# Scan of the even layer: order of VectorE's instructions within a step

## The reference, cut to what matters

```python
def rwkv7_scan(r, w, k, v, kk, bb, s0, reverse):
    def step(s, inp):
        r_t, w_t, k_t, v_t, kk_t, b_t = inp
        sa = jnp.einsum('bhij,bhj->bhi', s, kk_t)
        s = s * w_t[:, :, None, :] - sa[..., None] * b_t[:, :, None, :] + v_t[..., None] * k_t[:, :, None, :]
        return s, jnp.einsum('bhij,bhj->bhi', s, r_t)
...
    for d in range(2):
...
        s_ctx, yc = rwkv7_scan(*tc[:6], zeros, d == 1)
        _, yl = rwkv7_scan(*tl[:6], s_ctx, d == 1)
```

## Time and profile before

| | |
|---|---|
| median of 3 executions | 3216.98 us (3214.37 to 3218.5) |
| span of the profiled execution | 3213.7 us |
| TensorE, share of the span | 95% |
| VectorE | 54% |
| ScalarE | 36% |
| GpSimd | 42% |

### The profile page before, as it was taken

The page is one execution under the profiler, slowest core; times in us unless marked ns, Lnnn a source line. Parts: engine busy times, 40 slices in busy tenths (PEclk is TensorE's granted clock), DMA queues, the critical chain, the costliest instruction groups (busy, mean ns, idle before and its releaser), DMA issues. The chain is left out here.

```text
span 3213.7 us, 52487 instructions
## 1 busy us (share of the span) xinstructions
PE 3045.3 (95%) x20065; PEld 2461.7 (77%) x20065; DVE 1728.6 (54%) x3224; ACT 1155.9 (36%) x2075; POOL 1349.1 (42%) x893
## 2 busy tenths in 40 slices
PE   5999999899999999999999999999888889999998
PEld 4888876678887888877788887987666667778887
DVE  6445478654445566232666114537677754674443
ACT  3222235432223322234332223226544434435343
POOL 3444443244444434453434444224767660143332
PEclk8999999999999999999999999999999999999999
DMA  7655432155544554332255334213222233222222
GB/s 216 195 184 173 158 85 73 53 170 183 183 156 153 167 180 135 97 90 79 86 163 151 94 93 136 79 53 112 65 58 58 56 107 73 91 77 71 82 66 59
DMA packets 641381, 366.02 MB, mean 114 GB/s; under 512 B 107902, under 2 KB 634132, under 8 KB 640688
## 3 DMA queue, kind: packets, MB, share of 16 engines
q1 hardware_dynamic: 633216, 351.57, 37.2%
q10 hardware_dynamic: 6640, 10.49, 1.1%
q0 software_dynamic: 1344, 1.44, 0.2%
HBM read 334.27 MB, written 24.97 MB: 112 GB/s over the span
## 5 line engine op out<-in xcount | busy, mean ns | idle before, releaser
L270 POOL TENSOR_TENSOR w_lo<-w_raw,w_hi 128x1024 fp32r<-128x1024 f32 (+1 forms) x333 | 786.6, 2362 | 1316.6 <-ACT w_hi L262 1263.9
L335 PE MATMUL acc<-h,w_hi 128*128 128x512 f32 x2256 | 704.4, 393 | 0.0
L262 ACT ACTIVATE w_hi<-w_raw 128x1024 fp32r<-128x1024 f32 (+1 forms) x332 | 344.6, 1038 | 941.1 <-PE acc L335 687.9
L335 PEld LDWEIGHTS acc<-h,w_hi 128*128 128x128 f32 x2256 | 417.3, 188 | 84.6 <-issue 1.8
L335 PE MATMUL acc<-h,w_lo 128*128 128x512 f32 x1128 | 440.3, 390 | 0.0
L335 PE MATMUL acc<-hid,w_hi 128*128 128x512 f32 x1056 | 326.3, 390 | 0.0
L716 DVE SCALAR_TENSOR_TENSOR ada_part<-ada_raw,c_act,ada_part 128x256 f32<-128x256 f32 x672 | 315.0, 489 | 18.6
L335 PEld LDWEIGHTS acc<-h,w_lo 128*128 128x128 f32 x1128 | 211.7, 188 | 45.8
L335 PEld LDWEIGHTS acc<-hid,w_hi 128*128 128x128 f32 x1056 | 197.3, 188 | 40.7
L335 PE MATMUL spare<-h,w_hi 128*128 128x512 f32 x688 | 211.7, 389 | 0.0
L335 PE MATMUL acc<-hid,w_lo 128*128 128x512 f32 x528 | 205.6, 389 | 0.0
(11 more groups left out here) (700 smaller groups left out, 6094.7 us busy)
## 6 DMA issues: line engine op xcount, KB each, us to landing
w_raw<-in_ffn_w SPq DMA_DIRECT2D x240, 512.0 KB, 4.0
ada_raw<-in_ada_w SPq DMA_DIRECT2D x88, 1024.0 KB, 5.0
w_raw<-in_od_w_in SPq DMA_DIRECT2D x32, 512.0 KB, 4.0
w_raw<-in_ffn_w SPq DMA_DIRECT2D x32, 384.0 KB, 3.1
w_raw<-in_ev_w_in SPq DMA_DIRECT2D x22, 512.0 KB, 3.9
image<-inverse_wait SPq DMA_DIRECT2D x144, 64.0 KB, 2.1
first_ada<-in_ada_w SPq DMA_DIRECT2D x8, 1024.0 KB, 12.4
w_raw<-in_ab_w_in SPq DMA_DIRECT2D x16, 512.0 KB, 4.0
```

What stands on the lines that cost most here:

```text
L262: act.activation(K.w_hi[:, first % SPLIT, 0:tiles, :], K.raw[:, first % RAW, 0:tiles, :], ACT.Copy).then_inc(K.hi_ready, 1)
L270: pool.tensor_tensor(K.w_lo[:, first % SPLIT, 0:tiles, :], K.raw[:, first % RAW, 0:tiles, :], K.w_hi[:, first % SPLIT, 0:tiles, :].bitcast ...
L335: mm = pe.matmul(out, w[:, slot, k, :], moving(ap, k, tokens), start=first and k == 0 and p == 0, stop=last and k == tiles - 1 and p == le ...
```

## The change

`add` loses its spreading, which becomes a function of its own, `spread`. The waits and operands stay. In VectorE's `step` the spreading of direction 0 goes behind the two turned copies, that of direction 1 stays behind its `add`, and `between(3)` goes behind both. The other engines' queues stay as they are.

```diff
                     dve.tensor_tensor(oc, oc, V.low[:, 2 * P:3 * P], ALU.add).then_inc(V.ds, 1)
+
+                def spread(b, k, d):
+                    O, V = B[b % 3], U[d]
+                    ch = ORDER[d][k]
                     dve.wait_ge(V.ds, total(b, k, DS, 2))
                     dve.scalar_tensor_tensor(V.s.rearrange("p (h c) -> p h c", h=2), heads(V.sc), O.wlast[:, d, ch:ch + 1],
                                              K.bd64.rearrange("p (h c) -> p h c", h=2), ALU.mult,
...
                     between(2)
                     join(0)
                     join(1)
-                    between(3)
                     add(b, k, 0)
                     turn(0)
                     turn(1)
+                    spread(b, k, 0)
                     add(b, k, 1)
+                    spread(b, k, 1)
+                    between(3)
                     between(4)
                     between(5)
```

## The result

| | before | after |
|---|---|---|
| median of 5 executions | 3216.98 us | 3240.76 us (3238.99 to 3242.11) |
| span of the profiled execution | 3213.7 us | 3237.9 us |
| TensorE, share of the span | 95% | 94% |
| VectorE | 54% | 53% |
| granted clock of TensorE, mean from 2285 to 2725 us | 0.97 | 0.93 |

The ratio is 1.0074, with a 95% interval from 1.0063 to 1.0085: the change makes the kernel 23.8 us slower, against a forecast of 10.7. The sign was right; the time lies outside the range.

What follows compares the result with a forecast made beforehand. It took the ring of waits from TensorE to ScalarE to VectorE and back as the bound. Steps 1 to 4 +5.85, step 6 +4.7, reordering -1.4 and clock +1.5 made +10.65: 3227.6 us, range 3217 to 3236.

Steps and rivals of the forecast that it cites:

- Reordering alone: Spreading behind the turned copies: they come sooner, 0.18 us for each of 8 steps in blocks 5 and 6; -1.4 us.
- Step 1: First pass over k, blocks 1 to 4: ScalarE's square waits for moved kk, TensorE's take 1.5 us later.
- Step 2: Second pass over k: maximum and reciprocal moved, trailing work ends 0.92 us later; in block 3 idle time takes it.
- Step 6: Sixth pass over k: TensorE waits for the moved low copy; +1.5 us, in blocks 1 and 4 +0.87; sum +4.7.
- The grid: Rival: fifth pass's first spreading misses GpSimd's running operation, +1.8 us in each of blocks 1 to 4, 3234.8 us; chance 0.12.
- GpSimd waits for the inverse, longer in blocks 1 to 3: Expected sign: GpSimd's wait for VectorE's inverse, 1.87 us in block 3 before, gets longer in those blocks.
- Block 4's losses vanish in ScalarE's 3.40 us: Block 4: the 2.3 us lost in its first two passes vanish in ScalarE's wait for the inversion.
- the second rival: Mostly covered: losses of first two passes vanish in the inversion in blocks 1 to 3 too; 3220.3 us; chance 0.18.
- The clock: TensorE's slow-clock stretches behind standstills, some 1 us each, mainly first and sixth pass; +1.5 us, bounds -1.5 to +4.
- Step 3: Third pass over k: no piece in slot 3, ScalarE's gate activation stands ahead of its close; 0 us.
- steps 4 and 5: Fourth and fifth passes: a moved reciprocal frees TensorE's close, but GpSimd's run sets the rest; gain 0.1 us per block.

Runs made afterwards that it cites:

- Run 1: The changed kernel with between(3) back at its old place, so only the spreading moves; 3217.31 us, ratio 0.9996.
- experiment 4: The changed kernel with ScalarE's slot 4, the square of kk, behind its close in the first pass over k; 3229.09 us, ratio 1.0031.

## Why the prediction was off

- **Reordering alone, -1.4: right in size where it acts.** The plain steps of blocks 5 and 6 went from 9.96 to 9.78 us, the 0.18 forecast, and TensorE's `close` there has no wait left where the earlier trace rows had one. Run 1 then shows no gain in the median: the waits for images rose from 3.3 to 4.8 us there, and in blocks 1 to 4 step 6's gain went into the wait for the inversion. I had looked for giving back in the image waits only.
- **Step 1, +1.5 per block: right.** The distance from `join` to `take` grew by 1.66, 1.57, 1.56 and 1.57, the square waited 1.60 in block 1 and 1.50 in the others. That it is ScalarE's order is shown by experiment 4.
- **Step 2, +0.92: nearly right.** `take` came later by 1.15, 1.20 and 1.11 in blocks 1, 2 and 4, and 0.45 sooner in block 3.
- **Step 6, +1.5 and +0.87: the wait right, its size right in block 2 alone.** Block 2 has +1.51. Block 3, for which +1.5 was forecast too, has +0.72: there GpSimd's run now ends before the second spreading, which takes 0.35 us. Blocks 1 and 4 have +1.88 and +1.90, because the step "there some 0.65 us of waiting goes" took over from the kernel before that GpSimd has finished when the second spreading comes. But the same change had held GpSimd up (next point), so in the changed kernel it is still working: the spreading lasts 1.26 us and ends at 2364.36, behind GpSimd's end at 2364.22. What the Trainium skill says in SBUF — State Buffer, Who interferes with whom, that a VectorE operation with two SBUF inputs and a GpSimd operation that reads SBUF shut each other out, agrees with these ends. The grid that I feared for step 5 struck in step 6, at the very operation ahead of the moved copy.
- **"GpSimd waits for the inverse, longer in blocks 1 to 3": right.** In block 1 of the changed kernel:

```profile
2340.89 2.41 POOL L2301 TENSOR_TENSOR x<-x,x_context 128x768 f32<-128x768 f32 x1 [11.53 <-DVE x_context L2841]
```

  It was 1.87 us in block 3 before, and 8.10 after.
- **Block 4's losses vanish in ScalarE's 3.40 us: right in kind.** Steps 1 and 2 lost 5.55 us there, of which step 4 gave back 4.79, and the wait for the inversion fell from 4.1 to 0.7 in all. A cushion of this size took the 2.3 that I had put on it, but not the 5.55 that came. That blocks 1 to 3 would be covered too (the second rival) fell: their step 4 gave back 3.1 in all, 1.8 of it in block 1, where the kernel before happened to have a granted clock of 0.59 between 2332 and 2336 us.
- **The clock, +1.5: this is the step that failed.** The waits as such come to 6.4 (step 1), 3.0 (step 2) and 6.0 (step 6), less 2.7 for steps 1 and 2 of block 4, which are covered: 12.7 where I had 10.55 (5.85 + 4.7). The steps 1, 2 and 6 together lost 28.5 us, so 13.1 lie outside these waits. 5.9 of them are shown to be clock by experiment: the four steps 1 took 58.36 us, and with the six products 52.45. Of the rest no experiment filled a gap, but the rows tie it to the clock block by block: 4.8 in step 2, in blocks 1, 3 and 4, whose stretch behind `take` has 0.78, 0.62 and 0.78, and nothing in block 2 at 1.00; 2.5 in step 6, in blocks 1 and 4, at 0.75 where it was 0.85. That makes 13.2, all of what the waits leave over to a tenth, where the prediction had 1.5 for the clock. The prediction saw the mechanism and had its row (a `low` of 1.10 instead of 0.72 us behind a wait). But it counted the stretches that might come as net one or two of 1 us each, and set its upper bound at four. In the changed kernel there was one behind ScalarE's wait in all four blocks, at 1.3 to 1.6 us each, three in step 2 and two more in step 6. The clock also moved where nothing had changed: +2.3 us ahead of step 1 of block 1, at 0.67 against 0.80. Several of the other kernels show that same 22.8 us, run 1 (23.03) among them, others the 20.5; so it is no cost of the moved pieces.
- **Step 3, 0, and steps 4 and 5, -0.1 per block:** step 3 is right. Steps 4 and 5 together took 24.74, 23.04, 23.01 and 27.31 us before and 23.06, 23.11, 24.66 and 23.06 after, so the forecast is near in block 2 alone; blocks 1 and 4 gave more back, block 3 lost. Of step 5's +3.7, 1.6 is a stretch of slow clock in block 3 (0.88 over the step, 1.00 in the other three). No run was made for the rest, which stays open.
- **The range** ended at the grid rival's price and one stretch more. It gave the clock's term, for which the trace of before had a single row of the kind, no more room than the terms with rows of their own. The 3.3 us "around the span" are two things: 1.8 between time and span in one and the same execution (3239.73 and 3237.9 for the changed kernel), and the distance of the profiled execution from the median. The sum is the same.

## What to carry to other kernels

Moving work behind the critical updates helps only if nobody waits for it. For each moved piece, look up its reader on the other engines and what stands behind that reader in its queue: here a square that nobody needed soon stood ahead of ScalarE's `close`. Then price a new standstill of TensorE among small products at up to twice the wait itself (here 1.5 us of waiting and 1.3 to 1.6 us of clock), with room for it at every place and round though it will not come at each (10 of 12 here in step 1, 12 of 28 in step 2), and don't count that a gain stays until the second chain (here GpSimd's inversion) has been looked at.

## What the runs showed of the hardware

- After a standstill of 2.06 us among small products the granted clock was 0.50 for the next ones, and six otherwise useless 128x128 products (1.60 us) in the same gap kept it at 1.00. The Trainium skill (TensorE: Matmul & The Clock Gate, HAM oscillation — how this bites in real kernels) describes products that come back slow after each wait for data. This case agrees in kind, with a wait for ScalarE in the place of a transfer, but not in "each": twice in twelve the clock stayed at 1.00 behind a standstill of 1.90 us.
- One such product of 128x128 in f32 took 0.24 us (3.39 / 14), and in the shorter run 0.27 (1.60 / 6). I had planned with 0.12. The kernel's own 128x128 transposes (L2420 to L2422) start 0.11 us apart, but each of them is one instruction in the trace, and each of the added products is two (x28 for 14, x12 for 6).
- The same 128x128 spreading took 0.34 to 0.35 us beside an idle GpSimd and 1.26 us when one of GpSimd's 1.85 us operations was running.
